# Pooling product of a two-block transformer kernel: from full fp32 to high and low parts

## The chip, the cores and the metric

The kernel runs on one core of one Trainium2 chip. The metric is the time of one execution in microseconds (us) on the device, as the median of several runs. Before the change the median of three runs is 2799.16 us (2798.95 to 2802.92).

## What is computed

The reference runs two blocks of layers over a sequence of 1024 tokens of width 1024. The change touches only the beginning of the first one, where the six modulation vectors are computed and the multiscale pooling mixer runs:

```python
mod_x = s_c @ mod_w[i] + mod_b[i]                       # 1024 x 6144
sh1, sc1, g1, sh2, sc2, g2 = jnp.split(mod_x[:, None, :], N_MOD, axis=-1)
hx = x * (1.0 + sc1) + sh1
# multiscale_pool: for each of 4 groups of 256 channels, window w in (2, 4, 8, 16)
outs.append(centred_window_mean(hg, w) - hg)
y = jnp.einsum('blgc,gcd->blgd', p, w_group).reshape(B, L, D)
ox = y * scale
x = layer_norm(ALPHA * x + g1 * ox, ln_g[i, 0], ln_b[i, 0])
x = layer_norm(ALPHA * x + g2 * swiglu(x * (1.0 + sc2) + sh2, ...), ...)
```

Everything after it (the SwiGLU of the first block, then attention, mLSTM and the gated spatial layers of the second block) is untouched.

## The kernel before

The program is written out by hand: each engine has its own list of instructions in a fixed order, and the engines meet through semaphores. Channels lie on the 128 partitions, so the 1024 channels are eight tiles `k` of 128x1024, and each pooling group has two of them. P is 128, T is 1024, HALF is 512, KT is 8.

In the first 130 us these lists run side by side.

- **SyncE (the DMA queue, from L549).** It loads the parameters, the input in two halves of four tiles (`resid<-x_t`, L568), and the modulation weights in twelve blocks of 2 MB into three buffers `mod_big` (L569). Block n waits for the product of block n-3. Then come the first two slabs of the next layer's weights (`slab_raw<-w_in`, L572).
- **TensorE (from L1225).** `mod_block(n)` (L1236) multiplies a modulation block, `mod_columns(n)` (L1245) turns a row of results into columns, `pool_tile(j)` (L1258) makes output tile j of the pooling product, and `pool_means(j)` (L1150) adds up the means of the finished tile j. `pool_tile(j)` has four fp32 products 128x128 by 128x512. It reads the scaled weights `pw` and the window differences `acc` of group j // 2, and it waits for the addition of tile j-2 (`z_done`), because there are two banks in PSUM. `mod_block(n)` waits for `mod_read(n-1)`.
- **VectorE (from L2834).** `window(k)` (L2869) makes the window mean of tile k less the tile itself, by k // 2 + 1 additions of 128x1024 over a tree (L2879), one or two tiny corrections at the edges (L2888, L2890) and a last operation into `acc` (L2892). `pool_scale` and `pool_gate` (L2900 to L2913) make the small vectors from columns 1 and 3. `pool_add(j)` (L2928) adds the pooled tile j from PSUM, times its gain, to the residual stream.
- **ScalarE (from L1990).** `pad(k)` (L2010) copies a tile into a padded buffer, `scale_x(k)` (L2015) scales the residual, `scale_weights(g)` (L2022) scales the weights of a group, and `mod_read(n)` (L2002) copies a modulation row out of PSUM.
- **GpSimd (from L728).** After setting constants it does nothing until the first slabs have landed. It then splits them into a high and a low part (L752, L756).

From about 102 us on TensorE works with split operands: a product is three fp32r matmuls, high by high, high by low and low by high (`three`, L1072):

```python
pe.matmul(dst, w_h, r_h, start=first, stop=False, skip_group_check=True)
pe.matmul(dst, w_h, r_l, start=False, stop=False, skip_group_check=True)
return pe.matmul(dst, w_l, r_h, start=False, stop=last, skip_group_check=True)
```

Of the kernel before, what the change touches and what calls it, by code (L numbers as in the profile page):

```python
# [196 lines left out]
def build(nc, x_t, params, mod_w, pool_w, w_in, w_c, edges, w_spatial, b_spatial, out):  # L197
    with ExitStack() as ctx:
# [91 lines left out]

        take = overlay(work_base)
# [190 lines left out]
        px, p_sum, p_diff, px_step, p_done = beat("px"), beat("p_sum"), beat("p_diff"), beat("px_step"), beat("p_done")  # L482
        x_scaled, pool_mm, z_done = beat("x_scaled"), beat("pool_mm"), beat("z_done")
# [43 lines left out]
        m_ot, m_otr, m_so, m_g = beat("m_ot", 2), beat("m_otr", 2), beat("m_so", 2), beat("m_g")  # L527
# [22 lines left out]
        def _(sp):  # L550
# [11 lines left out]
            for n in range(MOD_BLOCKS):  # L562
                if n >= MOD_BUFFERS:
                    sp.wait_ge(mod_mm.sem, mod_mm.at(n - MOD_BUFFERS))
                if n in X_BEFORE:
# [4 lines left out]

            for s in range(2):
                sp.dma_start(raw[s][:], w_in[s]).then_inc(in_load[s].sem, 16)  # L572
# [10 lines left out]
            for s in range(2):  # L583
                sp.wait_ge(in_split.sem, in_split.at(FIRST_PAIR + s))
                load_ring(1, s, w_in, 2 + s, in_load[s])
            load_ring(1, C, w_c, 0, c_load)
# [139 lines left out]
        def _(pool):  # L726
# [21 lines left out]
            def split(n, slot, load, load_value, hi_done, used, done, fused=None):  # L748
# [5 lines left out]
                if fused is not None:  # L754
                    pool.wait_ge(n_fuse.sem, fused)
                pool.tensor_tensor(wlo[slot][:].rearrange("p k f -> p (k f)"), raw[slot][:], hi.bitcast(F32),  # L756
                                   ALU.subtract).then_inc(done.sem, 1)

# [309 lines left out]
        def _(pe):  # L1068
# [180 lines left out]
            def pool_tile(j):  # L1249

                g, e = j // 2, j % 2
                pe.wait_ge(p_done.sem, 2 * g + 2)
                pe.wait_ge(p_diff.sem, p_diff.at(2 * g + 1))
                if j >= 2:
                    pe.wait_ge(z_done.sem, j - 1)
                for t0 in (0, HALF):
                    for k in range(2):
                        mm = pe.matmul(pool_bank[e][:, t0:t0 + HALF], pw[:, g, k, e * P:(e + 1) * P],  # L1258
                                       acc[:, 2 * g + k, t0:t0 + HALF], start=(k == 0), stop=(k == 1),
                                       skip_group_check=True)  # L1260
# [16 lines left out]
            pe.wait_ge(lam_x.sem, lam_x.at(0))  # L1277
            pool_tile(0)
            mod_block(2)
# [712 lines left out]
        def _(act):  # L1992
# [24 lines left out]
            def scale_weights(g):  # L2017
# [3 lines left out]
                for k in range(2):  # L2021
                    act.activation(pw[:, g, k, :], pw[:, g, k, :], ACT.Copy, scale=sc1p[:, 2 * g + k:2 * g + k + 1]).then_inc(p_done.sem, 1)  # L2022

# [6 lines left out]
            for k in range(3):  # L2030
                scale_x(k)
            mod_read(0)
            pad(3)
            scale_x(3)
            mod_read(1)
# [3 lines left out]
            for g in range(1, 4):  # L2039
                scale_weights(g)  # L2040
            pad(6)
            for k in (4, 5):
                scale_x(k)
            mod_read(2)
            pad(7)
            scale_x(6)
            mod_read(3)
            scale_x(7)
# [1820 lines left out]
```

## Time and profile before

| | |
|---|---|
| median of 3 runs | 2799.16 us (2798.95 to 2802.92) |
| the profiled execution's own time | 2788.73 us |
| its span | 2787.0 us |
| mean granted TensorE clock | 0.996 of full speed |
| TensorE busy | 2691.3 us (97%) |
| VectorE, ScalarE, GpSimd busy | 54%, 37%, 50% |

The profile is of one execution. The span is the time from its first to its last instruction, and the execution's own time holds another 1.7 us around it. Times in the trace are in us from the start of the span.

### The profile page before, as it was taken

The page shows a single profiled execution, that of the slowest core. Times are in us where ns is not written, and L with a number is a line of the kernel's source. Part 1 is how long each engine was busy: PE and PEld are TensorE (multiplying, and loading weights), DVE is VectorE, ACT ScalarE, POOL GpSimd, SP SyncE. Part 2 cuts the span into 40 slices and gives each one's busy share as a digit, 9 for nine tenths or more (in the row PEclk, how much of TensorE's full clock was granted, in tenths as well). Part 3 has the DMA queues.
Part 4 walks back from the last instruction along what each step waited for, and adds up shares of the span by engine and source line. Part 5 has one row for each costly group of instructions (what it writes and reads, how often), then busy time and mean ns, then how long its engine had stood idle before and what let it go on. Part 6 is the DMA issues. An engine that isn't in the chain of part 4 may idle for free.

```text
span 2787.0 us, 39149 instructions
## 1 busy us (share of the span) xinstructions
PE 2691.3 (97%) x14084; PEld 2155.3 (77%) x14084; DVE 1506.5 (54%) x2237; ACT 1032.2 (37%) x1794; POOL 1388.4 (50%) x895
## 2 busy tenths in 40 slices
PE   7999999999999999999999999999989999999997
PEld 2588888888867777777777888888778878887885
DVE  6674544554475556655557654635475033336667
ACT  3642232222244433333333222231342165555342
POOL 0577677767643422122321334343244467877664
PEclk9999999999999999999999999999999999999999
DMA  9211111111112011001001111112222232223333
GB/s 387 100 52 52 53 46 60 53 45 57 49 54 76 25 32 37 30 30 38 30 24 37 49 51 46 52 45 61 76 107 104 85 106 90 75 83 129 128 114 137
DMA packets 67519, 202.25 MB, mean 73 GB/s; under 512 B 17620, under 2 KB 23892, under 8 KB 65256
## 3 DMA queue, kind: packets, MB, share of 16 engines
q1 hardware_dynamic: 46624, 169.46, 18.4%
q10 hardware_dynamic: 20808, 31.61, 3.3%
q8 instruction: 57, 0.93, 0.1%
q14 instruction: 30, 0.25, 0.0%
HBM read 171.61 MB, written 29.44 MB: 72 GB/s over the span
## 4 chain that ended last, share of the span: by engine, by line
PE 78%; POOL 8%; DVE 5%; DMA 4%; issue 3%; ACT 2%; POOLq 0%; SPq 0%; DVEq 0%; ACTq 0%
PE ps L1074 24%; PE ps L1076 23%; PE ps L1075 23%; POOL slab_lo L989 4%; DMA slab_raw<-w_in 2%; PE ps L1495 2%; PE ps L1506 1%; PE ps L1150 1%; POOL gu_lo L989 1%; DMA resid<-x_t 1%; PE ps L1258 1%; PE ps L1225 1%; POOL slab_raw L980 1%; POOL gu_s L978 1%; POOL gu_s L981 1%
## 5 line engine op out<-in xcount | busy, mean ns | idle before, releaser
L752 POOL TENSOR_TENSOR slab_hi<-slab_raw,zero 128x1024 fp32r<-128x1024 f32 x103 | 199.4, 1936 | 967.4 <-PE ps L1076 878.3
L1074 PE MATMUL ps<-h_hi,slab_hi 128*128 128x512 f32 x1616 | 642.6, 398 | 12.6 <-POOL h_lo L770 4.4
L1075 PE MATMUL ps<-h_lo,slab_hi 128*128 128x512 f32 x1616 | 631.5, 391 | 0.0
L1076 PE MATMUL ps<-h_hi,slab_lo 128*128 128x512 f32 x1616 | 631.1, 391 | 0.0
L1074 PEld LDWEIGHTS ps<-h_hi,slab_hi 128*128 128x128 f32 x1616 | 303.9, 188 | 90.1 <-issue 12.2
L1076 PEld LDWEIGHTS ps<-h_hi,slab_lo 128*128 128x128 f32 x1616 | 303.7, 188 | 66.1
L1075 PEld LDWEIGHTS ps<-h_lo,slab_hi 128*128 128x128 f32 x1616 | 304.0, 188 | 59.4
L756 POOL TENSOR_TENSOR slab_lo<-slab_raw,slab_hi 128x1024 fp32r<-128x1024 f32 x103 | 251.0, 2437 | 9.7 <-DVE mean L3139 1.7
L3065 DVE SCALAR_TENSOR_TENSOR resid<-ps,mod,resid 128x512 f32<-128x512 f32 x320 | 224.4, 751 | 0.5 <-issue 0.3
L817 POOL TENSOR_TENSOR slab_lo<-slab_raw,slab_hi 128x512 fp32r<-128x512 f32 x124 | 161.8, 1312 | 43.9 <-ACT slab_hi L2128 43.2
L1076 PE MATMUL ps<-t_hi,slab_lo 128*128 128x512 f32 x368 | 143.9, 391 | 0.0
L1075 PE MATMUL ps<-t_lo,slab_hi 128*128 128x512 f32 x368 | 143.8, 391 | 0.0
L1074 PE MATMUL ps<-t_hi,slab_hi 128*128 128x512 f32 x368 | 143.7, 391 | 0.0
L1074 PE MATMUL ps<-ffn_hi,slab_hi 128*128 128x512 f32 x352 | 139.1, 395 | 1.3 <-issue 1.3
L1076 PE MATMUL ps<-ffn_hi,slab_lo 128*128 128x512 f32 x352 | 140.1, 398 | 0.0
L817 POOL TENSOR_TENSOR slab_lo<-ffn_s,slab_hi 128x512 fp32r<-128x512 f32 x60 | 78.6, 1310 | 121.9 <-ACT slab_hi L2128 121.9
L1075 PE MATMUL ps<-ffn_lo,slab_hi 128*128 128x512 f32 x352 | 138.9, 395 | 0.0
L3046 DVE TENSOR_TENSOR ffn_p<-ps,ffn_p 128x512 f32<-128x512 f32 x20 | 13.8, 692 | 199.4 <-PE ps L1076 199.4
L3255 DVE TENSOR_TENSOR da_al<-ps,da_ah 128x512 fp32r<-128x512 f32 (+2 forms) x96 | 53.3, 555 | 121.8 <-ACT da_ah L2337 121.7
L1074 PE MATMUL ps<-slab_hi,h_hi 128*128 128x512 f32 (+1 forms) x320 | 111.9, 350 | 4.7 <-DVE h_lo L2972 4.7
L1075 PE MATMUL ps<-slab_lo,h_hi 128*128 128x512 f32 (+1 forms) x320 | 111.2, 347 | 0.0
L1076 PE MATMUL ps<-slab_hi,h_lo 128*128 128x512 f32 (+1 forms) x320 | 111.1, 347 | 0.0
(473 smaller groups left out, 5913.4 us busy)
## 6 DMA issues: line engine op xcount, KB each, us to landing
slab_raw<-w_in SPq DMA_DIRECT2D x168, 512.0 KB, 3.6
mod_big<-mod_w SPq DMA_DIRECT2D x12, 2048.0 KB, 12.4
slab_raw<-w_c SPq DMA_DIRECT2D x43, 512.0 KB, 3.6
res_scr<-resid ACTq DMA_DIRECT2D x4, 2048.0 KB, 7.2
resid<-res_scr ACTq DMA_DIRECT2D x2, 4096.0 KB, 13.3
gv_scr<-sg_t ACTq DMA_DIRECT2D x4, 2048.0 KB, 7.0
slab_raw<-gv_scr SPq DMA_DIRECT2D x16, 512.0 KB, 3.4
uz_scr<-gu_out SPq DMA_DIRECT2D x16, 512.0 KB, 4.7
```

The source lines that it names most:

```text
L752: pool.tensor_tensor(hi, raw[slot][:], zeros, ALU.add).then_inc(hi_done.sem, 1)
L756: pool.tensor_tensor(wlo[slot][:].rearrange("p k f -> p (k f)"), raw[slot][:], hi.bitcast(F32), ALU.subtract).then_inc(done.sem, 1)
L817: pool.tensor_tensor(ring(all_lo, f, b, j).rearrange("p k f -> p (k f)"), block_source(j), ring(all_hi, f, b, j).rearrange("p k f -> p (k ...
L978: pool.tensor_tensor(gu_s1[:], a21, gate_source(A22), ALU.add).then_inc(u_sum.sem, 1)
L980: pool.tensor_tensor(a21, gate_source(A11), a21, ALU.subtract).then_inc(u_sum.sem, 1)
L989: pool.tensor_tensor(low, gate_source(j), high.bitcast(F32), ALU.subtract).then_inc(u_lo.sem, 1)
L1074: pe.matmul(dst, w_h, r_h, start=first, stop=False, skip_group_check=True)
L1075: pe.matmul(dst, w_h, r_l, start=False, stop=False, skip_group_check=True)
L1076: return pe.matmul(dst, w_l, r_h, start=False, stop=last, skip_group_check=True)
L1495: mm = pe.matmul(score_bank[c][:, t0:t1], q[rows, cols], k[rows, t0:t1], start=(n == 0 and not diagonal), stop=(n == 2), skip_group_check= ...
L3065: dve.scalar_tensor_tensor(dst, PS[d % 2][:, half_of(e)], g2[:, d:d + 1], dst, ALU.mult, ALU.add)\
L3255: dve.tensor_tensor(a_lo[:, slots, :], turn_bank[:, 0:blocks * P].rearrange("p (b q) -> p b q", q=P), a_hi[:, slots, :].bitcast(F32), ALU. ...
```

## The change

Pooling product: four fp32 matmuls of a tile become twelve fp32r matmuls on high and low parts. The parts are new tiles: `pw_hi` and `acc_hi` (four buffers) are copies by ScalarE, `pw_lo` and `acc_lo` are subtractions by GpSimd, written over `pw` and `acc`. Two of the four buffers of `acc_hi` lie in the split slab of the third slot and one in its raw slab, so the load of that slab waits for the last pooling product. `mod_block(2)` now stands ahead of `pool_tile(0)`. On VectorE `pool_gate` and the first `pool_add` stand ahead of window 6, and the later additions are moved between the windows. SyncE issues the first two slabs ahead of modulation block 11 in place of behind it.

```diff
--- before.py
+++ after.py
@@ -288,6 +288,14 @@
         pw = take("pw", [P, 4, 2, 256])[0]
         edge = take("edge", [P, 32])[0]
 
+        pool_high = [h_base + (MOD_BUFFERS * KT + 2) * HALF * 4 + 4 * T * n for n in range(3)]
+        pw_hi = at_offset("pw_hi", [P, 4, 2, 256], F32R, pool_high[0])
+        pw_lo = at_offset("pw_lo", [P, 4, 2, 256], F32R, work_base + 7 * (4 * TP))
+        assert (4 * TP) % 32 == 0
+        acc_hi = [at_offset(f"acc_hi{n}", [P, T], F32R, at)
+                  for n, at in enumerate([base + 4 * T * at for at in (5, 8, 2)] + [pool_high[2]])]
+        acc_lo = at_offset("acc_lo", [P, KT, T], F32R, acc_base)
+
         take = overlay(work_base)
         sq = [take(f"sq{b}", [P, HALF])[0] for b in range(4)]
 
@@ -480,6 +488,7 @@
         mod_mm, mod_out, mod_turn, mod_col = beat("mod_mm"), beat("mod_out"), beat("mod_turn"), beat("mod_col")
         lam_mm, lam_x, dve_first = beat("lam_mm"), beat("lam_x", 2), beat("dve_first")
         px, p_sum, p_diff, px_step, p_done = beat("px"), beat("p_sum"), beat("p_diff"), beat("px_step"), beat("p_done")
+        p_wh, p_wl, p_ah, p_al = beat("p_wh"), beat("p_wl"), beat("p_ah"), beat("p_al")
         x_scaled, pool_mm, z_done = beat("x_scaled"), beat("pool_mm"), beat("z_done")
 
         n_mean_mm, n_mean, n_cent = beat("n_mean_mm", 2), beat("n_mean", 2), beat("n_cent", 2 * KT)
@@ -524,7 +533,7 @@
         m_s, m_am, m_ah, m_al = beat("m_s"), beat("m_am"), beat("m_ah"), beat("m_al")
         m_p, m_c, m_ch, m_cl, m_num = beat("m_p", 7), beat("m_c", 7), beat("m_ch", 7), beat("m_cl", 7), beat("m_num", 8)
         m_den, m_rd, m_hm = beat("m_den", 1 + 2 * NC), beat("m_rd", NC), beat("m_hm", NC)
-        m_ot, m_otr, m_so, m_g = beat("m_ot", 2), beat("m_otr", 2), beat("m_so", 2), beat("m_g")
+        m_ot, m_otr, m_so, m_g = after(p_ah, KT, 2), after(p_al, KT, 2), after(p_wh, 4, 2), after(p_wl, 4, 1)
         m_ss, m_std, m_r, m_n = beat("m_ss", 8), beat("m_std"), beat("m_r"), beat("m_n", 8)
         m_ntr, m_z, m_y, m_yh, m_yl = beat("m_ntr", 2), beat("m_z", 2), beat("m_y", 2), beat("m_yh", 2), beat("m_yl", 2)
         m_na = beat("m_na", NC // 2)
@@ -562,15 +571,15 @@
             for n in range(MOD_BLOCKS):
                 if n >= MOD_BUFFERS:
                     sp.wait_ge(mod_mm.sem, mod_mm.at(n - MOD_BUFFERS))
+                if n == MOD_BLOCKS - 1:
+                    for s in range(2):
+                        sp.dma_start(raw[s][:], w_in[s]).then_inc(in_load[s].sem, 16)
                 if n in X_BEFORE:
                     half = X_BEFORE.index(n)
                     tiles = slice(half * KT // 2, (half + 1) * KT // 2)
                     sp.dma_start(resid[:, tiles, :], x_t[:, tiles, :]).then_inc(x_ld[half].sem, 16)
                 sp.dma_start(mod_big[n % MOD_BUFFERS][:], mod_w[MOD_ORDER[n]]).then_inc(mod_ld[n % MOD_BUFFERS].sem, 16)
 
-            for s in range(2):
-                sp.dma_start(raw[s][:], w_in[s]).then_inc(in_load[s].sem, 16)
-
             def load_ring(f, slot, source, row, done):
                 sp.dma_start(raw[slot][:], source[bass.ds(row, 1)].rearrange("a p t -> p (a t)")).then_inc(done.sem, 16)
 
@@ -583,6 +592,7 @@
             for s in range(2):
                 sp.wait_ge(in_split.sem, in_split.at(FIRST_PAIR + s))
                 load_ring(1, s, w_in, 2 + s, in_load[s])
+            sp.wait_ge(pool_mm.sem, KT)
             load_ring(1, C, w_c, 0, c_load)
             def load_turn(f):
                 load_pair(f)
@@ -755,6 +765,29 @@
                     pool.wait_ge(n_fuse.sem, fused)
                 pool.tensor_tensor(wlo[slot][:].rearrange("p k f -> p (k f)"), raw[slot][:], hi.bitcast(F32),
                                    ALU.subtract).then_inc(done.sem, 1)
+
+            def weights_low(g):
+
+                pool.wait_ge(p_wh.sem, g + 1)
+                pool.tensor_tensor(pw_lo[:, g, :, :], pw[:, g, :, :], pw_hi[:, g, :, :].bitcast(F32), ALU.subtract)\
+                    .then_inc(p_wl.sem, 1)
+
+            def difference_low(k):
+
+                pool.wait_ge(p_ah.sem, k + 1)
+                pool.tensor_tensor(acc_lo[:, k, :], acc[:, k, :], acc_hi[k % 4][:].bitcast(F32), ALU.subtract)\
+                    .then_inc(p_al.sem, 1)
+
+            difference_low(0)
+            difference_low(1)
+            weights_low(0)
+            weights_low(1)
+            difference_low(2)
+            difference_low(3)
+            weights_low(2)
+            weights_low(3)
+            for k in range(4, KT):
+                difference_low(k)
 
             def split_in(n, slot, turn):
                 split(n, slot, in_load[slot], in_load[slot].at(turn), in_hi, in_mm, in_split)
@@ -1249,15 +1282,14 @@
             def pool_tile(j):
 
                 g, e = j // 2, j % 2
-                pe.wait_ge(p_done.sem, 2 * g + 2)
-                pe.wait_ge(p_diff.sem, p_diff.at(2 * g + 1))
+                pe.wait_ge(p_wl.sem, g + 1)
+                pe.wait_ge(p_al.sem, 2 * g + 2)
                 if j >= 2:
                     pe.wait_ge(z_done.sem, j - 1)
                 for t0 in (0, HALF):
                     for k in range(2):
-                        mm = pe.matmul(pool_bank[e][:, t0:t0 + HALF], pw[:, g, k, e * P:(e + 1) * P],
-                                       acc[:, 2 * g + k, t0:t0 + HALF], start=(k == 0), stop=(k == 1),
-                                       skip_group_check=True)
+                        mm = three(pool_bank[e][:, t0:t0 + HALF], pw_hi[:, g, k, e * P:(e + 1) * P], pw_lo[:, g, k, e * P:(e + 1) * P],
+                                   acc_hi[(2 * g + k) % 4][:, t0:t0 + HALF], acc_lo[:, 2 * g + k, t0:t0 + HALF], k == 0, k == 1)
                 mm.then_inc(pool_mm.sem, 1)
 
             def pool_means(j):
@@ -1275,8 +1307,8 @@
             mod_columns(0)
             mod_columns(1)
             pe.wait_ge(lam_x.sem, lam_x.at(0))
+            mod_block(2)
             pool_tile(0)
-            mod_block(2)
             mod_block(3)
             mod_columns(2)
             mod_columns(3)
@@ -2020,6 +2052,15 @@
                 act.wait_ge(mod_col.sem, 2)
                 for k in range(2):
                     act.activation(pw[:, g, k, :], pw[:, g, k, :], ACT.Copy, scale=sc1p[:, 2 * g + k:2 * g + k + 1]).then_inc(p_done.sem, 1)
+                act.wait_ge(p_done.sem, 2 * g + 2)
+                act.activation(pw_hi[:, g, :, :], pw[:, g, :, :], ACT.Copy).then_inc(p_wh.sem, 1)
+
+            def difference_high(k):
+
+                act.wait_ge(p_diff.sem, p_diff.at(k))
+                if k >= 4:
+                    act.wait_ge(pool_mm.sem, 2 * (k // 2 - 2) + 2)
+                act.activation(acc_hi[k % 4][:], acc[:, k, :], ACT.Copy).then_inc(p_ah.sem, 1)
 
             act.wait_ge(lam_mm.sem, 1)
             act.activation(shift_mean[:], PS[0][:, 2:3], ACT.Identity, scale=1.0 / D, bias=eps[:, 0:1]).then_inc(lam_x.sem, 1)
@@ -2029,25 +2070,38 @@
                 pad(k)
             for k in range(3):
                 scale_x(k)
+            difference_high(0)
             mod_read(0)
             pad(3)
             scale_x(3)
+            difference_high(1)
             mod_read(1)
             pad(4)
             scale_weights(0)
             pad(5)
-            for g in range(1, 4):
+            mod_read(2)
+            scale_weights(1)
+            difference_high(2)
+            pad(6)
+            difference_high(3)
+            for g in (2, 3):
                 scale_weights(g)
-            pad(6)
+            mod_read(3)
             for k in (4, 5):
                 scale_x(k)
-            mod_read(2)
             pad(7)
-            scale_x(6)
-            mod_read(3)
-            scale_x(7)
-            for n in range(4, 10):
-                mod_read(n)
+            for k in (6, 7):
+                scale_x(k)
+            difference_high(4)
+            difference_high(5)
+            mod_read(4)
+            mod_read(5)
+            difference_high(6)
+            mod_read(6)
+            mod_read(7)
+            difference_high(7)
+            mod_read(8)
+            mod_read(9)
             act.activation(warm[:], eps[:], ACT.Sqrt)
 
             def square(norm, n, src):
@@ -2931,14 +2985,16 @@
             for k in range(4):
                 window(k)
             pool_scale()
-            for k in range(4, 7):
-                window(k)
+            window(4)
+            window(5)
             pool_gate()
-            for j in range(2):
-                pool_add(j)
+            pool_add(0)
+            window(6)
+            pool_add(1)
+            pool_add(2)
             window(7)
-            for j in range(2, 5):
-                pool_add(j)
+            pool_add(3)
+            pool_add(4)
             modulation_part(5, SH1)
             dve.wait_ge(mod_col.sem, 4)
             chained(dve.tensor_tensor(mod[:, SH1], mod[:, SH1], mod[:, SH1], ALU.subtract))
```

GpSimd in the stretch between its constants and its first slab. `acc_lo` and `pw_lo` are the low parts, the number behind `acc_hi` is the buffer. Before, the constants are followed at once by the slabs:

```order
L743 AFFINE_SELECT causal<-causal 128x128
L752 TENSOR_TENSOR slab_hi<-slab_raw_49,zero 128x1024
L756 TENSOR_TENSOR slab_lo<-slab_raw_49,slab_hi 128x1024
```

And after the change:

```order
L753 AFFINE_SELECT causal<-causal 128x128
L778 TENSOR_TENSOR acc_lo<-acc,acc_hi_103 128x1024
L778 TENSOR_TENSOR acc_lo<-acc,acc_hi_104 128x1024
L772 TENSOR_TENSOR pw_lo<-pw,pw_hi 128x512 x2
L778 TENSOR_TENSOR acc_lo<-acc,acc_hi_105 128x1024
L778 TENSOR_TENSOR acc_lo<-acc,acc_hi_106 128x1024
L772 TENSOR_TENSOR pw_lo<-pw,pw_hi 128x512 x2
L778 TENSOR_TENSOR acc_lo<-acc,acc_hi_103 128x1024
```

Three more of the last kind follow, then the slabs. Twelve subtractions are new on this engine, all ahead of the slabs.

VectorE from the end of window 5 to the additions, before (`tree` are the stages of a window, `resid<-ps` is a `pool_add`):

```order
L2892 SCALAR_TENSOR_TENSOR acc<-tree_97,xpad_94 128x1024
L2879 TENSOR_TENSOR tree_95<-xpad_92 128x1039
L2879 TENSOR_TENSOR tree_96<-tree_95 128x1037
L2879 TENSOR_TENSOR tree_97<-tree_96 128x1033
L2879 TENSOR_TENSOR tree_98<-tree_97 128x1025
L2888 TENSOR_TENSOR tree_98<-tree_98,edge 128x8
L2890 TENSOR_TENSOR tree_98<-tree_98,edge 128x7
L2892 SCALAR_TENSOR_TENSOR acc<-tree_98,xpad_92 128x1024
L2900 TENSOR_TENSOR mod<-ps,par 128x8
L2913 TENSOR_TENSOR pool_gain<-mod,par 128x8
L2928 SCALAR_TENSOR_TENSOR resid<-ps,pool_gain,resid 128x1024 x2
```

And after:

```order
L2946 SCALAR_TENSOR_TENSOR acc<-tree_97,xpad_94 128x1024
L2954 TENSOR_TENSOR mod<-ps,par 128x8
L2967 TENSOR_TENSOR pool_gain<-mod,par 128x8
L2982 SCALAR_TENSOR_TENSOR resid<-ps,pool_gain,resid 128x1024
L2933 TENSOR_TENSOR tree_95<-xpad_92 128x1039
L2933 TENSOR_TENSOR tree_96<-tree_95 128x1037
L2933 TENSOR_TENSOR tree_97<-tree_96 128x1033
L2933 TENSOR_TENSOR tree_98<-tree_97 128x1025
L2942 TENSOR_TENSOR tree_98<-tree_98,edge 128x8
L2944 TENSOR_TENSOR tree_98<-tree_98,edge 128x7
L2946 SCALAR_TENSOR_TENSOR acc<-tree_98,xpad_92 128x1024
L2982 SCALAR_TENSOR_TENSOR resid<-ps,pool_gain,resid 128x1024 x2
```

The addition of tile 0 has moved ahead of window 6; the addition of tile 1 stays behind it.

## Rows read from the trace of the kernel before

**Rows 1.** The page: busy time of each engine over the span.
```profile
PE 2691.3 (97%) x14084; PEld 2155.3 (77%) x14084; DVE 1506.5 (54%) x2237; ACT 1032.2 (37%) x1794; POOL 1388.4 (50%) x895
```

**Rows 2.** Chain that ended last, first 260 us: start us, us, what.
```profile
2.68 23.25 DMA resid<-x_t
25.95 1.06 ACT xpad L2010
...
45.51 1.29 DVE resid L2928
46.94 3.67 PE ps L1258 x8
...
81.14 3.56 PE ps L1258 x8
```

**Rows 3.** Timeline of TensorE: start, us, engine line op, count [idle before].
```profile
24.59 2.07 PE L1245 MATMUL ps<-ones,mod_row 128*128 128x1 f32 x16
28.16 5.37 PE L1258 MATMUL ps<-acc,pw 128*128 128x512 f32 x8 [1.51 <-issue]
...
53.74 3.68 PE L1258 MATMUL ps<-acc,pw 128*128 128x512 f32 x8
```

**Rows 4.** Timeline of TensorE in the first split product after 102 us.
```profile
102.63 0.39 PE L1074 MATMUL ps<-h_hi,slab_hi 128*128 128x512 f32 x1
...
103.31 0.39 PE L1074 MATMUL ps<-h_hi,slab_hi 128*128 128x512 f32 x1
```

**Rows 5.** Timeline of VectorE in windows 2 to 6.
```profile
19.21 1.23 DVE L2892 SCALAR_TENSOR_TENSOR acc<-tree,xpad 128x1024 f32<-128x1024 f32 x1
21.41 1.24 DVE L2879 TENSOR_TENSOR tree<-xpad 128x1039 f32<-128x1039 f32 x1 [0.97 <-ACT xpad L2010]
...
24.34 1.23 DVE L2892 SCALAR_TENSOR_TENSOR acc<-tree,xpad 128x1024 f32<-128x1024 f32 x1
...
27.04 1.24 DVE L2879 TENSOR_TENSOR tree<-xpad 128x1039 f32<-128x1039 f32 x1
...
32.58 1.24 DVE L2879 TENSOR_TENSOR tree<-xpad 128x1039 f32<-128x1039 f32 x1
...
38.13 1.24 DVE L2879 TENSOR_TENSOR tree<-xpad 128x1039 f32<-128x1039 f32 x1
```

**Rows 6.** Timeline of GpSimd: the first slab, and two subtractions later.
```profile
83.60 1.89 POOL L752 TENSOR_TENSOR slab_hi<-slab_raw,zero 128x1024 fp32r<-128x1024 f32 x1 [77.96 <-DMA slab_raw<-w_in]
85.57 2.35 POOL L756 TENSOR_TENSOR slab_lo<-slab_raw,slab_hi 128x1024 fp32r<-128x1024 f32 x1
...
137.47 3.34 POOL L851 TENSOR_TENSOR t_lo<-t_raw,t_hi 128x512 fp32r<-128x512 f32 x2
```

**Rows 7.** Timeline of VectorE: an operation alone, then three beside GpSimd.
```profile
131.86 0.69 DVE L2987 TENSOR_TENSOR t_raw<-t_raw 128x512 f32<-128x512 f32 x1
...
136.17 5.19 DVE L2993 TENSOR_TENSOR t_raw<-t_raw 128x512 f32<-128x512 f32 x3
```

**Rows 8.** Timeline of VectorE with one operand in PSUM, beside the slab splits.
```profile
88.72 4.87 DVE L2954 TENSOR_TENSOR resid<-resid,ps 128x512 f32<-128x512 f32 x8 [2.72 <-PE ps L1183]
```

**Rows 9.** Timeline of ScalarE.
```profile
20.32 1.05 ACT L2010 ACTIVATE xpad<-resid 128x1024 f32<-128x1024 f32 x1
...
28.92 2.49 ACT L2022 ACTIVATE pw<-pw,sc1p 128x256 f32<-128x256 f32 x6
```

**Rows 10.** Windows: busy us per engine, granted clock, DMA share, GB/s.
```profile
20.00:40.00 20.00, 16.61 (x89) 7.06 (x90) 17.16 (x22) 15.21 (x22) 0.00 (x0) 0.91 1.01 428
```

**Rows 11.** Windows around a fall of the clock in a later stage.
```profile
1561.00:1564.00 3.00, 0.55 (x6) 0.32 (x3) 2.56 (x3) 1.94 (x2) 2.92 (x2) 1.00 0.01 3
1564.00:1567.00 3.00, 3.00 (x8) 2.38 (x9) 0.00 (x0) 0.00 (x0) 3.00 (x2) 0.55 0.03 5
```

**Rows 12.** DMA queue of SyncE, and the modulation blocks from issue to landing.
```profile
3.24 70.49 SPq L569 DMA_DIRECT2D mod_big<-mod_w x10
...
DMA to landing us min/median/max: 8.0/12.4/27.6
```

## The prediction

> **What bounds the kernel now.** I read the page first. TensorE is busy 97% of the span [rows 1], so a change elsewhere can only pay where TensorE waits, and a few microseconds lost ahead of the dense part are lost for good. The change lies entirely in the first 100 us, so I then followed the chain of waits there. Up to 26 us the chain is the transfer of the input's second half; from there to 46.8 us it is VectorE's windows 4, 5 and 6 and the addition of tile 0; from 46.94 us on it is TensorE alone, tile after tile [rows 2]. Tile 7 starts at 81.14 and ends at 84.70. From tile 2 to tile 7 are five steps in 81.14 - 46.94 = 34.20 us, 6.84 each: a pooling tile, the means of an older one, a modulation block and its columns. So two things set the end of this stage: when the tile additions let TensorE into its steps, and how long a step is. The number to follow is the end of tile 7; all that stands behind it (mean, variance, first split product) has the same operations as before and moves with it.
>
> **The products become shorter.** A tile takes 3.67 us [rows 2]. In the first split product three matmuls of 128x512 come in 103.31 - 102.63 = 0.68 us, 0.227 each, and the last one is counted 0.39 [rows 4]. Twelve of them take 11 x 0.227 + 0.39 = 2.89 us: 0.78 less. A step becomes 6.06 us. The modulation blocks still keep up: 2.1 MB at 428 GB/s [rows 10] is 4.9 us a block, and a block is asked for three steps before it is needed, against 8.0 us from issue to landing at best [rows 12]. If nothing else changed, the five steps and tile 7 would gain 6 x 0.78 = 4.7 us.
>
> **Where the additions go.** The addition of tile 0 no longer waits for window 6, but tile 3 needs two banks back, that is the additions of tiles 0 and 1, and the second still stands behind window 6. So the place to work out is the start of tile 3, at 53.74 before [rows 3]; its earliest start is when VectorE is through windows 0 to 6 and two additions.
>
> **What is new on the side engines.** ScalarE gets eight copies of 128x1024 (1.05 each by the copy into the padded tile) and four of 128x512 (about 0.6 each), 10.8 us in a stage where it has room, and 28.92 to 31.41 is six weight scalings, 0.41 each [rows 9]. GpSimd gets eight subtractions of 128x1024 and four of 128x512. It was idle for 77.96 us here. One of the large ones takes 2.35 us [rows 6]; the small ones I put at 1.29 (below). That is 8 x 2.35 + 4 x 1.29 = 24.0 us, and by GpSimd's own load it would all be hidden.
>
> **But it isn't hidden from VectorE.** The trace shows what happens when both engines work on operands in SBUF. An operation of VectorE on 128x512 takes 0.69 us alone, and three of the same size take 5.19 us, 1.73 each, while GpSimd makes two subtractions in 3.34, 1.67 each [rows 6, 7]. So they take turns: 1.73 is 0.69 plus nearly all of GpSimd's 1.29 (0.25 less than the sum), and the 1.29 itself is what one such subtraction takes with no rival, about half of the large one. With one operand in PSUM nothing is lost: eight centring operations beside the slab split take 4.87 us, 0.61 each [rows 8]. The Trainium skill says the same in "SBUF — State Buffer", section "Who interferes with whom": a VectorE instruction with two SBUF inputs and a GpSimd instruction that reads SBUF exclude each other for the whole instruction; by that rule the sum comes out as below, and the trace agrees with it. All stages of a window have two operands in SBUF; the additions of the pooled tiles read PSUM and are free of it.
>
> I therefore charge VectorE 2.35 - 0.25 = 2.10 us for each large subtraction that falls into its windows, and 1.04 for each small one.
>
> - Window 2 ends at 20.44 before [rows 5]. Low part 0 falls into it (ScalarE's copy is done at about 16.4 us, while window 2 begins at 16.3): 22.5.
> - Window 3 started at 21.41 after an idle 0.97 and ended at 25.57 [rows 5]. Now it starts at 22.5, low part 1 falls into it: 22.5 + 4.16 + 2.10 = 28.8. The small vector work takes it to 29.1, against 27.04 before.
> - Window 4 lasts 32.58 - 27.04 = 5.54 with its gap. The weights' low part 0 falls into it: 29.1 + 5.5 + 1.0 = 35.6.
> - Window 5 lasts 38.13 - 32.58 = 5.55. By its start ScalarE has handed over the weights of group 1 (about 35.2) and then the differences 2 and 3 and the weights of groups 2 and 3, so GpSimd always has one ready: two large and three small ones, 4.2 + 3.1 = 7.3 us. It ends at 35.6 + 5.5 + 7.3 = 48.4 instead of 38.0.
> - `pool_gate` is tiny but has two operands in SBUF, so low part 4 gets in ahead of it: +2.2, then 0.4 for itself: 51.0. The addition of tile 0 (1.29) [rows 2] ends at 52.3, 5.5 us later than before. Low part 5 holds window 6 until 53.1.
> - Window 6 lasts from 38.13 to about 44.9 before (the addition starts at 45.51, behind two tiny operations) [rows 2, 5], 6.7 us; nothing of GpSimd is left for it: 59.8. The addition of tile 1: 61.1. Tile 3 starts at 61.1, 7.4 us later than before.
>
> From there TensorE is alone again, since window 7 (61.1 + 1.3 + 6.7 + 2.1 = 71.2) and its low part (about 75) are ready before tile 6. Tile 7 ends at 61.1 + 4 x 6.06 + 2.89 = 88.2, against 84.70: **+3.5 us**.
>
> **The clock.** Before, TensorE had a hole from 26.66 to 28.16, and the mean clock from 20 to 40 us was 0.91 (2.4 GHz with a piece at 1.2): the first pooling tile took 5.37 us where later ones take 3.67 [rows 2, 3, 10]. Now there are more holes. `mod_block(2)` moved ahead of tile 0, and its block was asked for at 3.24 and landed 27.6 us later, at 30.8 [rows 12], so TensorE stands from 26.7 to 30.9; again for some 3 us before columns 3, because `mod_read(3)` stands behind four weight scalings and two copies on ScalarE; and before tiles 2 and 3. In a later stage, 3 us with TensorE busy for 0.55 were followed by 3 us at a mean clock of 0.55 [rows 11]. Such a piece of 3.4 us costs up to 1.7 us of TensorE's work where TensorE sets the pace. Ahead of tile 3 it mostly doesn't, since VectorE is later still. Ends: 0, and twice 1.7. I take 0.7, near the lower end, because most holes lie where tile 3 absorbs them.
>
> **Edits at nothing.** The slabs ahead of modulation block 11: GpSimd's splits end at about 94 instead of 92 and are needed at 102 + 4; block 11 is delayed by 1 MB, 2.5 us, and has some 9 us of slack. If that cover were gone it would cost at most those 2.5 us. The load of the third slot waits for tile 7 (88.2), but stands in the queue behind loads that wait for the splits anyway. `pool_tile(0)` behind `mod_block(2)` costs nothing for tile 3. 90 more matmul instructions on TensorE are the twelve-for-four of eight tiles.
>
> **Sum.** +3.5 + 0.7 = +4.2 us. Against the profiled execution's own 2788.73 this is 2792.9; the median of the runs lies 10.4 above that execution, and I carry the difference over: 2799.16 + 4.2 = **2803.4 us**.
>
> **The rivals.**
> - *The turns cost their full price, or the clock falls where TensorE leads: slower by more than 0.2%.* Ten low parts lie on VectorE's way to tile 3. If each costs all of its time instead of 0.25 less, that is 2.5 more: +6.7, 2805.9. One piece at half clock from tile 3 on adds 1.7 instead: +5.9 or so. It decides when tile 3 starts after 62.5 us. For it: window operations are chained, so that GpSimd can get in at each seam, and the tiny edge operations are seams too. Against it: the 0.25 was measured three times in a row. [...]
> - *No conflict on the windows (the change does what its order suggests).* Then tile 3 is bound by TensorE: ScalarE reaches `mod_read(3)` at about 41.5 (two pairs of weights with their copies and two copies later than `mod_read(2)`), columns 3 end at 42.6, tile 1 at 45.4, block 4 at 47.2, tile 2 at 50.1, tile 3 starts at 53.3 and tile 7 ends at 53.3 + 24.2 + 2.9 = 80.4: -4.3 us, 2794.9. For it: GpSimd's wait might fall into VectorE's gaps. Against it: rows 6 and 7.
> - *Faster by more than 0.2%.* Only if the steps behind tile 3 shrink too, by the slabs arriving earlier and TensorE's holes after 100 us closing: 4.7 for the products and a few more, 2792. I see no row for it.
>
> **How the numbers follow.** About 0.2% (5.6 us) is what a measurement of this kernel can tell from no change. My forecast, +1 to +5.6, gets 0.49; the slower rival 0.27; little or no conflict, -5.6 to +1, gets 0.18; faster beyond that 0.06. So faster 0.06, same 0.67, slower 0.27. The range reaches from the rival without conflict (2794.9) to the full price of the turns with one or two falls of the clock: 2794.5 to 2808.5.
>
> **What would show it.** Right: VectorE's window stages (1.24 us each) last 3 us or more between 36 and 48 us, and the sum of their time grows by more than 10 us; the first addition at about 51, tile 3 near 61, tile 7's end near 88; steps of 6.06. Wrong: window stages that keep 1.24 us beside GpSimd, or tile 3 at 54 or before; a fp32r tile well above 2.9 us; or a step that waits for a modulation block.

## The result and the profile after

The changed kernel takes 2804.57 us in the median of 20 runs (2797.82 to 2808.03) against 2797.51 (2788.12 to 2803.49) for the kernel before, run beside it. The ratio is 1.0023 with a 95% interval of 1.0015 to 1.0030: slower by 4 to 8 us. The profiled execution has a span of 2803.9 us, against 2787.0. That overstates the difference, because the execution of before that was profiled lay 9 to 10 us below the median of its kernel.

The page of the changed kernel, the same line as [rows 1]:

```profile
PE 2696.4 (96%) x14116; PEld 2167.6 (77%) x14116; DVE 1518.8 (54%) x2237; ACT 1039.4 (37%) x1806; POOL 1422.5 (51%) x907
```

GpSimd has 12 more instructions and 34 us more busy time; VectorE has no more instructions, yet 12.3 us more. TensorE has 32 more: the trace counts each fp32 matmul as two, so a tile goes from 8 to 12. VectorE's timeline in windows 2 to 6 of the changed kernel shows why, beside [rows 5]:

```profile
17.88 3.28 DVE L2933 TENSOR_TENSOR tree<-tree 128x1037 f32<-128x1037 f32 x1
...
30.55 3.46 DVE L2933 TENSOR_TENSOR tree<-tree 128x1037 f32<-128x1037 f32 x2
...
35.77 1.24 DVE L2933 TENSOR_TENSOR tree<-xpad 128x1039 f32<-128x1039 f32 x1
37.05 5.51 DVE L2933 TENSOR_TENSOR tree<-tree 128x1037 f32<-128x1037 f32 x2
42.60 2.22 DVE L2942 TENSOR_TENSOR tree<-tree,edge 128x4 f32<-128x4 f32 x1
44.85 1.21 DVE L2944 TENSOR_TENSOR tree<-tree,edge 128x3 f32<-128x3 f32 x1
46.10 2.27 DVE L2946 SCALAR_TENSOR_TENSOR acc<-tree,xpad 128x1024 f32<-128x1024 f32 x1
...
48.68 1.28 DVE L2982 SCALAR_TENSOR_TENSOR resid<-ps,pool_gain,resid 128x1024 f32<-128x1024 f32 x1
49.88 3.18 DVE L2933 TENSOR_TENSOR tree<-xpad 128x1039 f32<-128x1039 f32 x1
53.10 5.82 DVE L2933 TENSOR_TENSOR tree<-tree 128x1037 f32<-128x1037 f32 x3
...
60.50 2.47 DVE L2982 SCALAR_TENSOR_TENSOR resid<-ps,pool_gain,resid 128x1024 f32<-128x1024 f32 x2
```

A stage that takes 1.24 us alone lasts 3.28 when it has to wait for a large subtraction of GpSimd. A tiny operation at the edge, 0.16 us alone, lasts 2.22 or 1.21. The addition of tile 0, which reads one of its operands from PSUM, keeps its 1.28. GpSimd's timeline beside it:

```profile
38.13 6.67 POOL L778 TENSOR_TENSOR acc_lo<-acc,acc_hi 128x1024 fp32r<-128x1024 f32 x2
44.76 2.53 POOL L772 TENSOR_TENSOR pw_lo<-pw,pw_hi 128x512 fp32r<-128x512 f32 x2
49.56 5.73 POOL L778 TENSOR_TENSOR acc_lo<-acc,acc_hi 128x1024 fp32r<-128x1024 f32 x2 [2.28 <-ACT acc_hi L2063]
```

TensorE's timeline at tile 3, where the two kernels part for good (before: 53.74, 3.68 us for the whole tile [rows 3]):

```profile
55.36 1.05 PE L1278 MATMUL ps<-ones,mod_row 128*128 128x1 f32 x8
61.92 0.77 PE L1107 MATMUL ps<-acc_hi,pw_hi 128*128 128x512 f32 x1 [5.51 <-DVE resid L2982]
62.48 0.63 PE L1108 MATMUL ps<-acc_lo,pw_hi 128*128 128x512 f32 x1
...
66.75 0.63 PE L1109 MATMUL ps<-acc_hi,pw_lo 128*128 128x512 f32 x1
67.31 1.00 PE L1183 MATMUL ps<-resid,ones 128*32 128x128 f32 x16
```

It waited 5.51 us for the addition of tile 1, and then the tile ran at 1.2 GHz, 5.4 us long. The windows of the same execution (the columns of [rows 10]) have the clock at full for the first part of the hole, and at half (0.50) for the rest of it and through the whole tile:

```profile
57.00:58.00 1.00, 0.00 (x0) 0.00 (x0) 0.96 (x2) 0.00 (x0) 0.00 (x0) 0.92 0.88 311
58.00:61.00 3.00, 0.00 (x0) 0.00 (x0) 2.90 (x5) 0.00 (x0) 0.00 (x0) 0.50 0.93 339
...
62.00:65.00 3.00, 3.00 (x7) 2.37 (x8) 2.97 (x3) 0.00 (x0) 0.00 (x0) 0.50 0.25 98
65.00:67.00 2.00, 2.00 (x6) 1.32 (x4) 1.93 (x3) 0.00 (x0) 0.00 (x0) 0.50 0.00 0
...
68.00:69.00 1.00, 1.00 (x19) 0.30 (x15) 0.93 (x3) 0.53 (x1) 0.39 (x1) 0.96 0.07 16
```

From tile 4 on a step (a pooling tile, the means of an older one, a modulation block and its columns) is 6.17 us. Before it was 6.82 by the starts of tiles 3 to 7 in the timeline; the prediction's 6.84 is from the chain. Tile 7 ends at 92.4 us instead of 84.7.

### The profile page after: what moved, and what is told of

Same layout as the page of the kernel before. It is cut to its first block, busy times and chain, and to the rows that moved or that the text cites. A ratio compares the mean times of both kernels' runs of the same rounds, so it can differ in the third digit from the quotient of the medians.

```text
span 2803.9 us, 39259 instructions
## 1 busy us (share of the span) xinstructions
PE 2696.4 (96%) x14116; PEld 2167.6 (77%) x14116; DVE 1518.8 (54%) x2237; ACT 1039.4 (37%) x1806; POOL 1422.5 (51%) x907
## 4 chain that ended last, share of the span: by engine, by line
PE 80%; POOL 6%; DVE 6%; DMA 3%; issue 3%; ACT 2%; POOLq 0%; DVEq 0%; SPq 0%; ACTq 0%
PE ps L1107 25%; PE ps L1109 24%; PE ps L1108 24%; POOL slab_lo L1022 3%; PE ps L1527 2%; DMA slab_raw<-w_in 2%; DVE tree L2933 1%; PE ps L1183 1%; PE ps L1538 1%; PE ps L1258 1%; PE ps L1929 1%; POOL gu_lo L1022 1%; POOL slab_raw L1013 1%; POOL gu_s L1011 1%; POOL gu_s L1014 1%
```

## The experiments

The theory to test: VectorE and GpSimd take turns when both read operands in SBUF, this delays the first two additions of pooled tiles, and TensorE pays for it twice, by waiting and by its clock. All ratios are to the kernel before, run beside each version. The end of tile 7 is read from each version's TensorE timeline, one execution each; it is 84.7 before and 92.4 after. Of each edit the main lines are shown; "..." stands for the rest.

**GpSimd's subtractions left out.** The products read the high part where they read the low one.

```diff
-            difference_low(0)
-            difference_low(1)
...
-                pe.wait_ge(p_wl.sem, g + 1)
-                pe.wait_ge(p_al.sem, 2 * g + 2)
+                pe.wait_ge(p_wh.sem, g + 1)
+                pe.wait_ge(p_ah.sem, 2 * g + 2)
```

> The changed kernel without GpSimd's twelve subtractions: the products read the high part in place of the low one, so the low parts are left out and the output is not the reference's; TensorE does the same twelve matmuls a tile. Theory (taking turns): VectorE's window stages of 128x1024 all go back to 1.24 us, window 5 ends before 39 us instead of 48.3, the addition of tile 1 ends before 55, and tile 3 is then bound by TensorE's own list (53 to 57 us instead of 61.9); tile 7 ends at 81 to 84.5, that is 8 to 11 us earlier than in the changed kernel, and the time is 0.9980 to 1.0000 of before. Rival (the products wait for a chain ScalarE to GpSimd, or for the read of modulation row 3 on ScalarE, not for VectorE): window stages of up to 5.5 us stay, or tile 3 still starts at 60 or later.

Measured: 0.9991 (0.9981 to 1.0001). Groups of VectorE's instructions from 10 to 70 us, first in the changed kernel, then in this one:

```profile
L2933 DVE TENSOR_TENSOR tree<-tree 128x1037 f32<-128x1037 f32 x6 | 14.5, 2420 | 0.2
L2933 DVE TENSOR_TENSOR tree<-tree 128x1033 f32<-128x1033 f32 x4 | 7.9, 1981 | 0.1
L2942 DVE TENSOR_TENSOR tree<-tree,edge 128x4 f32<-128x4 f32 x2 | 2.4, 1193 | 0.1
```

```profile
L2923 DVE TENSOR_TENSOR tree<-tree 128x1037 f32<-128x1037 f32 x6 | 7.4, 1241 | 0.2
L2923 DVE TENSOR_TENSOR tree<-tree 128x1033 f32<-128x1033 f32 x4 | 4.9, 1236 | 0.1
L2932 DVE TENSOR_TENSOR tree<-tree,edge 128x4 f32<-128x4 f32 x2 | 0.3, 161 | 0.1
```

Every stage is back at its own time, the addition of tile 1 ends at 53.4, tile 3 starts at 56.3 straight behind TensorE's own work, and tile 7 ends at 83.8. With all the matmuls and all of ScalarE's copies in place the loss is gone. It also shows the second limit: even with no conflict only 0.9 us is left of the gain at tile 7, because columns 3 came late. TensorE stood for 2.64 us before them, and VectorE's gate, which needs the same columns, for 5.98 us:

```profile
42.88 1.05 PE L1268 MATMUL ps<-ones,mod_row 128*128 128x1 f32 x8 [2.64 <-ACT mod_row L2024]
```

```profile
43.97 0.17 DVE L2944 TENSOR_TENSOR mod<-ps,par 128x8 f32<-128x8 f32 x1 [5.98 <-PE ps L1268]
```

Those columns wait for the read of modulation row 3, which stands behind the copies and weight scalings on ScalarE. Tile 1 behind them took 4.6 us, in part at 1.2 GHz (the mean clock from 43 to 49 us was 0.72), and from there TensorE's own list leads to tile 3. VectorE's wait holds nothing up here.

**GpSimd busy as long, but only writing.**

```diff
...
-                pool.tensor_tensor(acc_lo[:, k, :], acc[:, k, :], acc_hi[k % 4][:].bitcast(F32), ALU.subtract)\
-                    .then_inc(p_al.sem, 1)
+                for part in range(2):
+                    pool.memset(acc_lo[:, k, :].bitcast(F32), 0.0).then_inc(p_fill.sem, 1)
+                    pool.wait_ge(p_fill.sem, 2 * k + part + 1)
+                pool.memset(acc_lo[:, k, 0:HALF].bitcast(F32), 0.0).then_inc(p_al.sem, 1)
```

> GpSimd works as long as in the changed kernel, but only writes: in place of each subtraction of differences it sets the low part to zero two and a half times over (about 2.4 us), in place of each of the weights once. So the low parts are left out and the output is not the reference's. Theory (turns because both read SBUF operands): nothing is lost, window stages stay at 1.24 us and tile 3 starts as in the kernel without subtractions, at 53 to 57. Rival (GpSimd at work of any kind slows VectorE): stages of 3 us beside it, tile 3 at 60 to 62.

Timelines of GpSimd and of VectorE in window 2 of this version:

```profile
16.57 1.96 POOL L779 MEMSET acc_lo<- 128x1024 f32 x2 [10.96 <-ACT acc_hi L2065]
18.59 0.52 POOL L781 MEMSET acc_lo<- 128x512 f32 x1
```

```profile
17.84 1.24 DVE L2935 TENSOR_TENSOR tree<-tree 128x1037 f32<-128x1037 f32 x1
```

GpSimd writes from 16.57 to 19.11, and the stage beside it keeps 1.24 us, where the changed kernel has 3.28. Tile 3 starts at 57.7 and tile 7 ends at 85.3. From 10 to 70 us the stages of all windows keep a mean of 1.23 to 1.24 us. (The writes in place of the weights' subtractions are shorter than those were, 0.53 us, and the 2.5 us of a large one are three instructions of at most 1 us.) So it is not that GpSimd works, but that it reads. (One execution, 2792.68 us, gives no ratio.) The Trainium skill, "SBUF — State Buffer", section "Who interferes with whom", says just this, that a GpSimd instruction which only writes is outside the conflict.

**TensorE kept running before tile 3**, by 44 matmuls of 256 columns into an unused piece of PSUM.

```diff
             for j in range(2, KT):
+                if j == 3:
+                    for _ in range(44):
+                        pe.matmul(BANK[3][:, 256:512], pw_hi[:, 0, 0, 0:P], pw_hi[:, 0, 1, :], start=True, stop=True,
+                                  skip_group_check=True)
                 pool_tile(j)
```

> The changed kernel with 44 matmuls of 256 columns into an unused piece of PSUM ahead of tile 3, where TensorE stood for 5.5 us. Theory (tile 3 ran at 1.2 GHz because TensorE had stood): the granted clock is 1.00 in tile 3, its twelve matmuls take 2.8 us instead of 5.3, tile 3 still starts at 61.9 and tile 7 ends at 89.7 instead of 92.3; the time is 2.5 us below that of the changed kernel, 1.0005 to 1.002 of before. Rival (the clock fell for another reason): tile 3 still takes 5 us or more.

Measured: 1.0012 (1.0000 to 1.0023). The interval overlaps that of the changed kernel, so the times alone don't separate the two; the trace does. Windows of this version at tile 3:

```profile
61.90:65.00 3.10, 3.06 (x16) 2.28 (x20) 3.07 (x3) 0.00 (x0) 0.00 (x0) 1.00 0.33 137
```

Tile 3 starts at 61.95 as before the edit and takes 3.0 us instead of 5.4. Tile 7 ends at 90.5 and not at 89.7: TensorE's columns 6 now waited 0.73 us for VectorE, because the subtraction of difference 6, asked for earlier, fell into window 7. The clock's share of the loss is thus 2.4 us at tile 3 and 1.9 at tile 7, in one execution.

**Only the order of VectorE, with the fp32 products.**

```diff
-            for k in range(4, 7):
-                window(k)
+            window(4)
+            window(5)
             pool_gate()
-            for j in range(2):
-                pool_add(j)
+            pool_add(0)
+            window(6)
+            pool_add(1)
+            pool_add(2)
             window(7)
...
```

> The kernel before, its fp32 products kept, with the order of VectorE alone changed as in the change (gate and first addition ahead of window 6). Theory: tile 2 is then bound by TensorE at 45.3 and tile 3 by the addition of tile 1 behind window 6, at 52.1 instead of 53.7; tile 7 ends at 83.0 instead of 84.7, ratio 0.9994. Rival (the order itself costs, because the addition of tile 1 now waits for window 6 alone): tile 3 later than 53.7.

Measured: 0.9994 (0.9982 to 1.0005), not told apart from no change. Tile 3 starts at 53.4, not at 52.1: the first tile was slower in this execution (6.4 us against 5.4, more of it at 1.2 GHz), and everything on TensorE moved with it. Tile 7 ended at 84.4, not at 83.0. No cost of the order shows, and no gain either.

**Two moves undone: the slabs loaded last again, tile 0 ahead of block 2 again.**

> The changed kernel with two of its moves undone: the first slabs are again loaded behind modulation block 11, and tile 0 stands again ahead of modulation block 2. Theory (both cost nothing): tile 3 starts at 61 to 62 and tile 7 ends at 91 to 93 as in the changed kernel, ratio 1.0015 to 1.003. Rival (they carry part of the loss, through the holes and the clock, or part of a gain): tile 7 ends more than 1.5 us earlier or later.

Measured: 1.0021 (1.0009 to 1.0033), as the changed kernel. But tile 3 started at 64.8, not 61 to 62, and tile 7 ended at 93.3, just outside the 91 to 93 expected. TensorE worked at 1.2 GHz through tile 0, and the next modulation read came late, so that ScalarE stood for 8.39 us:

```profile
40.70 0.60 ACT L2034 ACTIVATE mod_row<-ps 128x512 f32<-128x512 f32 x1 [8.39 <-PE ps L1269]
```

With high and low parts, tile 0 in first place waits for ScalarE and GpSimd (it starts at 33.35, where before it started at 28.16) and holds modulation block 2 up. With the change's own order tile 7 ended 0.9 us earlier, but two executions of one program can differ by more than that here, and the ratio shows nothing.

**The low parts made by VectorE**, between its windows, none by GpSimd.

```diff
+            difference_low(0)
             window(3)
+            difference_low(1)
             pool_scale()
             window(4)
+            weights_low(0)
             window(5)
+            weights_low(1)
+            difference_low(2)
+            difference_low(3)
             pool_gate()
...
```

> The changed kernel with the twelve low parts made by VectorE itself (1.24 us for a large one, 0.69 for a small one, placed between its windows) and none by GpSimd. Theory: the loss was GpSimd's slower operation (2.35 and 1.29 us) held against VectorE's windows, so VectorE doing the same work is cheaper: window 5 ends near 40, gate at 43, the addition of tile 1 ends near 53, tile 3 starts at 54 to 57 bound by TensorE, tile 7 ends at 82 to 85; ratio to before 0.998 to 1.000. Rival (the low parts are too much work for this stage wherever they are made): tile 3 at 60 or later, ratio 1.001 or more.

Measured: 1.0011 (1.0002 to 1.0020), outside what the theory asked for. No stage was stretched, and tile 3 started at 58.3, earlier than the changed kernel's 61.9 but later than the 54 to 57 expected. Tile 5 then started only at 73.9. TensorE's timeline there:

```profile
72.77 1.29 PE L1256 MATMUL ps<-ones,mod_row 128*128 128x1 f32 x8 [3.00 <-DVE mod L2932]
```

I had put the small vector work on column 5 behind the last low part, and TensorE's columns 6 wait for it. With those lines ahead of low parts 6 and 7 (the addition of tile 4 moves too, behind low part 6):

> Low parts by VectorE as in the run before, but the small vector work on modulation column 5 placed ahead of the low parts of differences 6 and 7. There, columns 6 waited 3 us behind the last low part, because TensorE waits for that small work, and tile 5 then ran at 1.2 GHz. Theory: with that gone the hole before tile 5 is gone too, tile 5 starts at 70.6 instead of 73.9, tile 7 ends at 86 or before (90.6 in that run, 84.7 before), ratio to before 0.9990 to 1.0005, 5 us below the earlier form. Rival (low parts on VectorE cost as such): tile 7 at 89 or later, ratio 1.001 or more.

Measured: 0.9993 (0.9984 to 1.0001), tile 7 ends at 85.5. So with the same twelve subtractions on VectorE, and the small vector work in its place, the whole loss of the change (1.0023) is gone, though VectorE has more work of its own. No gain is told apart from no change.

**High and low parts for tiles 4 to 7 alone**, GpSimd starting when window 6 is done. More than that differs from the changed kernel: tile 0 stands ahead of modulation block 2 again, and ScalarE's list is near that of the kernel before. VectorE's order and the slabs' place are those of the change.

```diff
+            pool.wait_ge(p_diff.sem, p_diff.at(6))
+            difference_low(4)
+            difference_low(5)
+            weights_low(2)
+            weights_low(3)
+            pool.wait_ge(p_diff.sem, p_diff.at(7))
+            difference_low(6)
+            difference_low(7)
...
+                        if g < 2:
+                            mm = pe.matmul(pool_bank[e][:, t0:t0 + HALF], pw[:, g, k, e * P:(e + 1) * P],
+                                           acc[:, 2 * g + k, t0:t0 + HALF], start=(k == 0), stop=(k == 1),
+                                           skip_group_check=True)
+                            continue
```

> Fp32 products as before for tiles 0 to 3, high and low parts only for tiles 4 to 7; GpSimd starts its subtractions only when window 6 is done, so that none lies on VectorE's way to tile 3; VectorE's new order kept. Theory: tile 3 starts at 52 as with the order alone, the subtractions of tiles 4 and 5 stretch window 7 by 4 to 7 us, for which there is room, and from tile 4 on a step is 6.1 us instead of 6.8: tile 7 ends at 80 to 80.5 instead of 84.7, ratio 0.9983 to 0.999, below both kernels. Rival (the four split tiles still wait): tile 4 starts after 59.5 or tile 6 after 72, ratio 0.9995 or more.

Measured: 0.9972 (0.9962 to 0.9982), clearly below both kernels. VectorE pays in window 7, where three stages take 7.71 us instead of 3.77, and nobody waits for it:

```profile
52.41 7.71 DVE L2934 TENSOR_TENSOR tree<-tree 128x1037 f32<-128x1037 f32 x3
```

Tile 3 starts at 52.6, tile 4 at 59.4, a step is then 6.17, and tile 7 ends at 81.0, 3.7 us earlier than before. The time fell by 0.0028 of 2798, that is 7.8 us, more than the 3.7. Two more runs asked where the rest is from.

> The version with high and low parts for tiles 4 to 7 alone once more, the same program on another day's chip. Theory: 3.7 us less at tile 7 and no more behind it, so 0.9975 to 0.9990. Rival: 0.9970 or less again, then something behind tile 7 gives 4 us more.

Measured: 0.9970 (0.9958 to 0.9982), as the rival had it. And tile 7 ended at 83.4 in this execution of the same program, not at 81: its first tile took longer, and tile 3 started at 55.1.

> The version with high and low parts for tiles 4 to 7 alone, with the first slabs loaded behind modulation block 11 as before. That version measured 0.9972, 7.8 us below before, of which the stage up to tile 7 explains 3.7. Theory (the slabs' place costs and gives nothing; the rest is spread of the measurement): tile 7 ends at 81, ratio within 0.0010 of the same version run beside it. Rival (the earlier slabs give the other 4 us): ratio 0.9985 or more here and 0.9972 beside it.

Measured: 0.9976 (0.9965 to 0.9987), within 0.0010 of the other: the slabs' place is not it. But here too tile 7 ended later than the 81 expected, at 84.0.

**The kernel before, profiled twice more.**

> The kernel before, unchanged, profiled once more. The times of seven versions against before came out 1.3 to 4 us lower than the ends of tile 7 in their profiles against the one profile of before, whose own time, 2788.73, lies 10 us below the median. Theory (that one execution of before was a fast one): here the input's second half lands later than 25.9, tile 7 ends 1 to 3 us after 84.7, or a piece at 1.2 GHz falls between 97 and 112 us as in most of the other versions; own time 2793 or more. Rival (before always runs this stage so): tile 7 at 84.5 to 85 and no such piece.

> The kernel before a third time, as the run beside it: the same expectations, to see how far two executions of one program lie apart at the end of tile 7.

Tile 7 ended at 84.75 and 85.01, so that stage repeats. But both had the piece at 1.2 GHz that the first profile lacked. Windows of the second profile of before, where the first has 1.00 from 97 to 112:

```profile
97.00:101.00 4.00, 3.52 (x55) 3.04 (x53) 3.65 (x7) 3.64 (x6) 1.84 (x2) 1.00 0.02 4
101.00:104.00 3.00, 2.57 (x8) 2.12 (x9) 2.71 (x5) 2.26 (x5) 2.36 (x3) 0.50 0.00 0
104.00:108.00 4.00, 4.00 (x17) 2.39 (x16) 3.64 (x5) 3.83 (x6) 2.45 (x3) 0.52 0.00 0
```

Their own times were 2797.84 and 2802.19. With three profiles each of the kernel before and of the late split (the third with the slabs last) the two can be set side by side, at tile 3, at tile 7 and at ScalarE's first table load, where the dense part has begun:

| | tile 3 starts | tile 7 ends | table load |
|---|---|---|---|
| before | 53.74, 53.81, 54.07 | 84.7, 84.75, 85.01 | 134.56, 137.34, 136.49 |
| late split | 52.60, 55.13, 55.72 | 81.0, 83.4, 84.0 | 132.25, 134.94, 135.62 |

What repeats is the time from the start of tile 3 to the end of tile 7: 30.9 us in each profile of before, 28.3 to 28.4 in each of the late split. So 2.6 us are the shorter products of four tiles. In two of the three the late split gives a part of that back, because tile 3 starts later. On the mean it is 2.0 us ahead at tile 7 and 1.9 at the table load, of the 7 to 8 measured. The other 5 or 6 us are not explained; an interval is about 3 us to either side, so it doesn't cover them. Further on, single executions of one program drift apart by as much, and not by the clock alone: between the table loads at 2254.61 and 2543.65 us of the first profile of before, the second loses 4.6 us more at a granted clock of 1.00 in both. Why the late split should fare better there, no run shows.

The changed kernel reaches its table load at 143.61 us, 6.3 and 7.1 us behind the two later profiles of before and 9.05 behind the first. That is the size of the measured loss, so nothing behind this stage is needed to explain it.

## Why the prediction was right

The forecast was +4.2 us (2803.4), the measured ratio is +6.4 (1.0023) and the median of the changed kernel is 2804.57, inside 2794.5 to 2808.5. The mechanism was the one forecast: VectorE and GpSimd take turns, tile 3 starts late, and the shorter products win only part of it back. The size was less good: a loss of 0.23% lies just past the 0.2% that I had put between "same" (0.67) and "slower" (0.27), so it fell into the slower rival's bin.

- **Turns on SBUF.** Charged 2.10 us for a large subtraction and 1.04 for a small one; the trace has 3.28 - 1.24 = 2.04 and 2.22 - 0.16 = 2.06, and 1.21 - 0.16 = 1.05. Window 5 was to end at 48.4, it ended at 48.4. That this is the cause is shown by the run without subtractions and by the one that only writes.
- **Order behind window 5.** The gate did not wait for low part 4, as I had it: the copy of difference 4 came from ScalarE only at 49.4, behind the gate, the addition of tile 0 ended at 50.0 instead of 52.3, and the two large subtractions fell into window 6 instead. There they cost 4.0 us, where I had counted 3.0 around the gate. The two errors nearly cancelled, which is luck: tile 3 was to start at 61.1 and started at 61.92.
- **Steps.** 6.06 forecast, 6.17 measured; a fp32r tile takes 3.03 against my 2.89, since the matmuls followed each other at 0.23 and the first one behind other work took 0.32. Four steps and the last tile make 0.6 us.
- **The clock.** This is the term that was mis-sized: 0.7 forecast, 2.4 at tile 3 measured (5.4 against 3.0 us). I took the lower end because most holes lay where tile 3 absorbs them. But the hole that mattered was the one directly ahead of tile 3, and the clock did not come back until the tile was done: I had counted a piece of 3.4 us, and this one lasted from 57.8 to 68.1. With 2.4 the sum would have been +5.9, and the tile end +7.7 comes from 0.8 (start of tile 3), 2.4 + 0.4 (clock, with the means behind it) and 0.6 (steps) on top of the +3.5.
- **Edits at nothing.** The slabs' place made no difference (0.9976 beside 0.9970). With both moves undone the ratio stayed (1.0021). The "90 more matmul instructions" are 32 in the trace; nothing in the sum hangs on it.
- **The rival "full price of the turns, or the clock falls where TensorE leads".** Its second half happened, its first did not: a turn cost 0.24 to 0.31 us less than the sum of both operations (3.28 against 1.24 + 2.35, 2.22 against 0.16 + 2.35, 1.21 against 0.16 + 1.29), and tile 3 started before the 62.5 that was to decide for it.
- **The rival without conflict.** Without the subtractions tile 7 ended at 83.8, not 80.4: tile 1 started 1.2 us later than I had it (43.8), and I had left the clock out of that case: the tile took 4.6 us, largely at 1.2 GHz.

## What to carry to other kernels

Work given to an idle GpSimd is not free if it reads SBUF while VectorE has two SBUF operands: charge VectorE nearly the full time of each such instruction, and put them where VectorE is not what the others wait for. Here the same split, restricted to the four tiles behind the last window on TensorE's path, with tile 0 and ScalarE's list put back, turned +0.23% into -0.24% to -0.30% in three series. Of those 7 to 8 us the traces show 2.6 as shorter products; the rest is measured and not explained. A hole in TensorE's work can cost more than its length, since the work behind it may run at half the clock: here 5.5 us of waiting were followed by a tile that took 2.4 us longer. Count that for the hole directly ahead of work on the path. And when one profile of a version looks ahead by a few microseconds, take a second one: the late split's first profile was the best of three.

## What the runs showed of the hardware

- A tiny VectorE operation is as good a seam as a large one: operations of 0.16 us waited 2.06 and 1.05 us for GpSimd.
- In the changed kernel the clock came back late: it was at half from 57.8 to 68.1 us, with TensorE working without a break from 61.92 on. Kept at work through the same hole, TensorE had 1.00 all along.
- The same program falls to 1.2 GHz in different places: the late split's first tile took 6.2 us in one execution and 6.7 in another, the columns ahead of it 1.95 and 3.57, and tile 3 started 2.5 us apart (52.6 and 55.1). One profile is good to 2 or 3 us in this stage, so a smaller difference between two profiles shows nothing by itself.
